# First loads from two queues, four square buffers and earlier splits in a one-core float32 encoder trunk

## The chip, the core and the metric

The kernel runs on one core of a Trainium2 chip. The time is the device time of one execution in microseconds (us). The profile is of one execution; its engines are PE (TensorE, the matrix engine), PEld (its weight loads), DVE (VectorE), ACT (ScalarE), POOL (GpSimd) and SP (SyncE, which here only issues transfers). A "q" behind an engine's name is its instruction queue, for instance SPq for the transfers that SP issues.

## What is computed

Two layers on 272 tokens (16 learned tokens ahead of 256) of width 1024, all in float32. Each layer is a half-step SwiGLU network, a mixer, and a second half-step SwiGLU network, each wrapped in two RMS norms. The mixer of the first layer is attention, that of the second a gated recurrence:

```python
for layer in range(2):
    g = norm_gains[layer]
    h = h + 0.5 * rms_norm(swiglu(rms_norm(h, g[0]), ffn_w_in[layer, 0], ffn_w_out[layer, 0]), g[1])
    hn = rms_norm(h, g[2])
    m = attention_mixer(hn, ...) if layer == 0 else recurrent_mixer(hn, ...)
    h = h + rms_norm(m, g[3])
    h = h + 0.5 * rms_norm(swiglu(rms_norm(h, g[4]), ffn_w_in[layer, 1], ffn_w_out[layer, 1]), g[5])
return h[:, 16:]
```

The recurrent mixer projects to a gate and to `xr`, runs a convolution of four taps over the tokens (`xc = conv_b + sum(xp[:, j:j + L] * conv_w[j])`), forms gates from `xc`, scans in both directions and projects back with `rec_w_out`.

## The kernel before

**Layout.** `h` lies transposed, 8 chunks of 128 features by 272 tokens. Each engine has its own program, written out by hand in the order in which it is to run, and semaphores join them; there is no scheduler. The program's blocks are `block.sync` (SP), `block.tensor` (PE), `block.scalar` (ACT), `block.vector` (DVE) and `block.gpsimd` (POOL).

**Products.** A float32 product is made of three matmuls (`product`, L508 to L510): weights and activations are each split in a rounded high part and a rest. ACT writes the high part of a weight unit (`high`, L1092, from `raw` to `wh`), DVE the rest (`low`, L1591, to `wl`), and then PE may use the unit. A unit is 1 MB (8 x 256 columns), there are four slots of `raw`, `wh` and `wl`, and SP loads a unit as soon as DVE has split what was in its slot. Activations are split in the same way: `xh` by ACT (`x_high`, L1098), `xl` by DVE (`low_x`, L1597).

**The start.** SP loads the tokens in six transfers, the left 512 columns ahead of the right 512 (`tokens(half)`, L432 to L434), and between and behind them the first weight unit in a quarter, a quarter and a half (L396), then unit after unit (L381). ACT's queue loads the learned tokens, the identity (`cst`) and the norm gains (L1528 to L1530). PE runs 13 products on zeros (L1059), transposes the tokens chunk by chunk (L1069; the gains, L1073, after the second chunk) into four banks, and then begins the first unit (`first_tiles`, L564 to L569, and the second unit at L547 to L550). ACT and DVE copy the transposed chunks to `h` (`take_h` L1537, `copy_h` L2154), split the unit in parts (`high_part` L1543, `low_part` L2150) and the activations.

**The end of a sub-layer.** The output projection ends in tiles of 128 features. For each, ACT squares it (`sqb`, two buffers) and scales it with the gain (`mg`), and DVE adds the squares up (`add_squares`, L1614, to `acc`). A square waits until the buffer is free, so for the addition two tiles back. The last square is not added by DVE: `mean_of_projection` (L970) multiplies `acc` and the last square with a matrix of 1/1024. ACT takes the root (`root_of_projection`, L1150), DVE adds the result to `h` (`residual`, L1641 to L1645). `mg_first` splits the first chunk of the scaled tile early (ACT L1108, DVE L1620), so that PE has work while the norm is finished (`first_chunk`, L527 to L531 for the second part of it). POOL multiplies `h` back by an older root in between (`restore`, L2205), and the root of the projection waits for that.

**Attention's output projection** (`projection(1, ...)`) has four units; DVE's turns are in `projection`: two additions, then a `low` of the next sub-layer's units. **The recurrent mixer** works through twelve units in the order of `REC_ORDER` ("x" and "e" are columns of `rec_w_in`, "g" gates); `conv` has 8 operations for a block of 256 features, two for each tap. **Its output projection** (`recurrent_out`) works in the order of `ROUT_PLAN`: tiles 0 to 5 by halves, then tiles 6 and 7, all in banks that ACT reads tile by tile; a tile from 4 on waits until ACT has emptied the tile that shared its bank.

Of the kernel before, what the change touches and what calls it, by code (L numbers as in the profile page):

```python
# [9 lines left out]
ALU = mybir.AluOpType  # L10
ACT = mybir.ActivationFunctionType
# [53 lines left out]
ROUT_SPLIT = 2  # L65
ROUT_PLAN = [(c, 0, 2) for c in range(KC)] + [(c, 2, 4) for c in range(KC)] + [(c, 4, 6) for c in range(6)] + [(c, 6, 8) for c in range(6)] + [(6, 4, 8), (7, 4, 8)]
# [88 lines left out]
def build(nc, x, meta, gains, ffn_in, ffn_out, w_qkv, q_gain, k_gain, w_o, rec_in, conv_w, conv_b,  # L155
          gate_w, gate_b, lam, rec_out, consts, out):
    ctx = ExitStack()
    with ctx:  # L158
# [108 lines left out]
        gates_used = sem("gates_used")  # L267
        xc_rounded, xc_split = sem("conv_rounded"), sem("conv_split")
# [3 lines left out]
        s_xin = [sem("left_tokens_landed"), sem("right_tokens_landed")]  # L272
# [87 lines left out]

        def conv_parts(n):

            v = split_a if n == 0 else split_b
            return v[:, 0], v[:, 1]
# [10 lines left out]
        def _(sp):  # L375
# [7 lines left out]
            def ffn(n):  # L383
# [45 lines left out]
            def tokens(half):  # L429

                cols = slice(D // 2 * half, D // 2 * half + D // 2)
                sp.dma_start(tok_in[META:TT, 0, cols], x[0:TT - META, cols]).then_inc(s_xin[half], 16)  # L432
                sp.dma_start(tok_in[0:TT, 1, cols], x[TT - META:2 * TT - META, cols]).then_inc(s_xin[half], 16)
                sp.dma_start(tok_in[0:L - 2 * TT, 2, cols], x[2 * TT - META:SEQ, cols]).then_inc(s_xin[half], 16)  # L434

# [10 lines left out]

            ffn(0)
# [55 lines left out]
        def _(pe):  # L503
# [582 lines left out]
        def _(act):  # L1086
# [320 lines left out]
            def recurrent():  # L1407
                def unit_high(what, freed, units):
                    high(U_REC + REC_ORDER.index(what), 0, KC, freed, units)

                def conv_high(n):
# [59 lines left out]
                unit_high("g1", (xr_done, 4), 1)  # L1471
# [794 lines left out]
```

## Time and profile before

| What | us |
|---|---|
| median of 3 runs | 1040.99 |
| lowest and highest | 1040.65, 1041.19 |
| the profiled execution | 1041.22 |
| its span from first to last instruction | 1039.3 |
| PE busy in the span | 1023.8 |
| DVE, ACT, POOL busy | 708.7, 562.5, 64.0 |

The profiled execution took 1.9 us more than its span, which lies before the first and behind the last instruction. Times in rows are counted from the start of the span. A row of the timeline is: start, length, engine, line, operation, tile written and tiles read, shape, count; in brackets the engine's idle time before it and what ended it. Consecutive instructions of one kind are merged to a row. A queued instruction's row can begin a little before its predecessor's ends, since engines are pipelined.

### The profile page before, as it was taken

How to read it: one execution, taken by the hardware profiler on the slowest of the kernel's cores; microseconds unless marked ns; L12 is line 12 of the kernel's file. 1: busy time of each engine (PE TensorE's matmuls, PEld its weight loads, DVE VectorE, ACT ScalarE, POOL GpSimd, SP SyncE). 2: the span in 40 equal slices, each digit the busy share in tenths (PEclk: the TensorE clock that was granted, in tenths of full speed). 3: DMA queues.
4: the chain of work that ended last, by engine and by line, in shares of the span. 5: the costliest groups of instructions: out<-in, count | busy, mean ns of one | idle time of the engine just before them, and what ended most of it. 6: DMA issues, size and time to landing. Idle time of an engine off the chain costs nothing. (4 is left out here: it accounts for less than half of the span.)

```text
span 1039.3 us, 20522 instructions
## 1 busy us (share of the span) xinstructions
PE 1023.8 (99%) x8308; PEld 999.9 (96%) x8308; DVE 708.7 (68%) x1040; ACT 562.5 (54%) x834; POOL 64.0 (6%) x62
## 2 busy tenths in 40 slices
PE   8999999999999999999999999999999999999997
PEld 8999999999889999999999999999999999999886
DVE  6766656488868866655478666654899987676652
ACT  6554454467875644445465444444679865544641
POOL 0000000008004000002100000030000030000000
PEclk9999999999999999999999999999999999999999
DMA  9754446635204355535655654367453736556531
GB/s 294 240 178 161 147 149 205 211 111 174 69 1 163 123 174 187 181 116 190 205 163 162 195 170 141 114 207 226 123 167 97 264 95 208 184 179 233 179 118 41
DMA packets 158175, 170.16 MB, mean 164 GB/s; under 512 B 3344, under 2 KB 150088, under 8 KB 158104
## 3 DMA queue, kind: packets, MB, share of 16 engines
q1 hardware_dynamic: 157720, 168.70, 50.1%
q8 instruction: 51, 0.84, 0.4%
q0 software_dynamic: 96, 0.28, 0.1%
q10 hardware_dynamic: 288, 0.18, 0.1%
q14 instruction: 20, 0.16, 0.1%
HBM read 167.82 MB, written 1.05 MB: 162 GB/s over the span
## 5 line engine op out<-in xcount | busy, mean ns | idle before, releaser
L1591 DVE TENSOR_TENSOR wl<-raw,wh 128x2048 fp32r<-128x2048 f32 (+3 forms) x166 | 346.6, 2108 | 141.5 <-ACT wh L1092 141.2
L508 PE MATMUL bank<-xh,wl 128*128 128x272 f32 (+1 forms) x1492 | 431.6, 289 | 0.2 <-DVE tmp L1707 0.2
L510 PE MATMUL bank<-xh,wh 128*128 128x272 f32 (+1 forms) x1492 | 428.5, 287 | 0.0
L509 PE MATMUL bank<-xl,wh 128*128 128x272 f32 (+1 forms) x1492 | 427.0, 286 | 0.0
L1092 ACT ACTIVATE wh<-raw 128x2048 fp32r<-128x2048 f32 (+2 forms) x165 | 284.2, 1746 | 104.5 <-PE bank L510 83.8
L508 PEld LDWEIGHTS bank<-xh,wl 128*128 128x128 f32 x1492 | 281.1, 188 | 2.1 <-issue 1.2
L510 PEld LDWEIGHTS bank<-xh,wh 128*128 128x128 f32 x1492 | 281.1, 188 | 0.0
L509 PEld LDWEIGHTS bank<-xl,wh 128*128 128x128 f32 x1492 | 281.0, 188 | 0.0
L509 PE MATMUL bank<-al,wh 128*128 128x272 f32 x528 | 152.2, 288 | 0.0
L508 PE MATMUL bank<-ah,wl 128*128 128x272 f32 x528 | 152.2, 288 | 0.0
L510 PE MATMUL bank<-ah,wh 128*128 128x272 f32 x528 | 151.4, 287 | 0.0
L1179 ACT ACTIVATE tmp<-tmp 128x272 f32<-128x272 f32 (+1 forms) x88 | 37.5, 428 | 207.6 <-DVE tmp L1706 207.4
L509 PEld LDWEIGHTS bank<-al,wh 128*128 128x128 f32 x528 | 99.3, 188 | 0.0
L510 PEld LDWEIGHTS bank<-ah,wh 128*128 128x128 f32 x528 | 99.2, 188 | 0.0
L508 PEld LDWEIGHTS bank<-ah,wl 128*128 128x128 f32 x528 | 99.2, 188 | 0.0
L1725 DVE TENSOR_TENSOR al<-tmp,ah 128x272 f32 (+3 forms) x88 | 38.2, 438 | 51.1 <-ACT ah L1184 50.5
L2205 POOL TENSOR_TENSOR h<-h,root 128x272 f32<-128x272 f32 (+1 forms) x32 | 39.4, 1267 | 538.5 <-DVE root L1630 409.6
L1706 DVE TENSOR_TENSOR tmp<-bank,r 128x272 f32<-128x272 f32 (+1 forms) x88 | 38.1, 433 | 46.1 <-PE bank L510 46.0
L1184 ACT ACTIVATE ah<-tmp 128x272 f32 (+3 forms) x88 | 37.4, 429 | 47.4 <-DVE tmp L1715 47.4
L1715 DVE TENSOR_TENSOR tmp<-tmp 128x272 f32<-128x272 f32 (+1 forms) x88 | 38.2, 438 | 13.6 <-ACT tmp L1179 10.1
L547 PE MATMUL bank<-xh,wl 128*128 128x272 f32 (+1 forms) x152 | 39.4, 287 | 0.2 <-DVE wl L2150 0.2
L548 PE MATMUL bank<-xh,wh 128*128 128x272 f32 (+1 forms) x152 | 39.3, 286 | 0.0
(246 smaller groups left out, 1191.2 us busy)
## 6 DMA issues: line engine op xcount, KB each, us to landing
raw<-in_ffn_w_in SPq DMA_DIRECT2D x87, 1024.0 KB, 5.8
raw<-in_ffn_w_out SPq DMA_DIRECT2D x24, 768.0 KB, 4.7
raw<-in_ffn_w_out SPq DMA_DIRECT2D x24, 640.0 KB, 3.9
raw<-in_ffn_w_out SPq DMA_DIRECT2D x10, 1024.0 KB, 5.0
raw<-in_rec_w_in SPq DMA_DIRECT2D x8, 1024.0 KB, 5.4
raw<-in_attn_w_qkv SPq DMA_DIRECT2D x6, 1024.0 KB, 5.0
raw<-in_attn_w_o SPq DMA_DIRECT2D x4, 1024.0 KB, 5.5
raw<-in_rec_gate_w SPq DMA_DIRECT2D x16, 256.0 KB, 3.7
```

What stands on the lines that cost most here:

```text
L508: pe.matmul(dst, b, mh, start=first, stop=False)
L509: pe.matmul(dst, a, ml, start=False, stop=False)
L510: return pe.matmul(dst, a, mh, start=False, stop=last)
L547: pe.matmul(dst, b, xh[:, k, t0:L], start=k == 0, stop=False)
L548: pe.matmul(dst, a, xh[:, k, t0:L], start=False, stop=False)
L1092: act.activation(wh[:, slot(u), 0:kn * 256], raw[:, slot(u), 0:kn * 256], ACT.Copy).then_inc(wh_ready, units)
L1179: act.activation(sl[:, b, t0:L], gp[:, b, t0:L], ACT.Silu).then_inc(silu_done, 1)
L1591: dve.tensor_tensor(wl[:, slot(u), 0:kn * 256], w, wh[:, slot(u), 0:kn * 256].bitcast(F32), ALU.subtract).then_inc(w_ready, units)
L1706: dve.tensor_tensor(gp[:, b, t0:L], bank[banks[0]][:, t0:L], r[:, t0:L], ALU.mult).then_inc(gate_scaled, 1)
L1715: dve.tensor_tensor(aa[:, b, t0:L], sl[:, b, t0:L], up[:, b, t0:L], ALU.mult).then_inc(a_full, 1)
L1725: dve.tensor_tensor(d, aa[:, b, t0:L], s, ALU.subtract).then_inc(a_ready, 1)
L2205: pool.tensor_tensor(h[:, c, t0:L], h[:, c, t0:L], root[:, t0:L], ALU.mult).then_inc(h_restored, 1)
```

## The change

**Start.** The tokens come in three transfers of whole rows ahead of all else on SP, under one semaphore. The first two quarters of the first unit move to ACT's queue, behind the identity and ahead of the gains. ACT and DVE split these quarters ahead of their copies of the transposed tokens (DVE's second quarter behind its third copy, and its fourth copy ahead of the first `low_x`).

**Attention's projection.** `mg_first` moves from the last turn to the second on ACT and DVE; DVE adds square 6 ahead of its last `low`.

**Convolution.** The first tap of the blocks 0 and 1 is made by ACT (`first_tap`), and DVE splits the gates' unit ahead of the other taps.

**Output projection of the recurrence.** Squares go through four buffers (two of `sqb`, two of `pad`), so that a square waits for the addition four tiles back; POOL begins its `restore` when the first output tile is done and not when the last product of scan and gate is.

```diff
+        def rout_square(m):
+
+            return (sqb[:, m % 2] if m % 4 > 1 else pad[:, m % 2, 0:L])[:, PROJ_T0[4]:L]
...
                 if n == 0:
-                    for k0, k1, done in ((0, 2, quarter_landed[0]), (2, 4, quarter_landed[1]), (4, 8, landed[0])):
-                        if k0 < 4:
-                            tokens(k0 // 2)
-                        sp.dma_start(raw[:, 0, 256 * k0:256 * k1].rearrange("p (k c) -> p k c", k=k1 - k0),
-                                     vin[:, k0:k1, 0:256]).then_inc(done, 16)
+                    sp.dma_start(raw[:, 0, 256 * 4:256 * 8].rearrange("p (k c) -> p k c", k=4), vin[:, 4:8, 0:256]).then_inc(landed[0], 16)
...
+            sp.dma_start(tok_in[META:TT, 0, :], x[0:TT - META, :]).then_inc(s_xin, 16)
+            sp.dma_start(tok_in[0:TT, 1, :], x[TT - META:2 * TT - META, :]).then_inc(s_xin, 16)
+            sp.dma_start(tok_in[0:L - 2 * TT, 2, :], x[2 * TT - META:SEQ, :]).then_inc(s_xin, 16)
             ffn(0)
...
                 if c == 0:
-                    pe.wait_ge(s_xin[0], 64)
-                if c == 4:
-                    pe.wait_ge(s_xin[1], 48)
+                    pe.wait_ge(s_xin, 64)
...
             def projection(pj, u0):
                 for g in range(4):
-                    if g == 3:
-                        mg_first(pj)
                     square_tile(pj, 2 * g, PROJ_BANKS[pj][g][0])
                     square_tile(pj, 2 * g + 1, PROJ_BANKS[pj][g][1])
+                    if g == 1:
+                        mg_first(pj)
...
+                def first_tap(n):
+
+                    act.wait_ge(xr_scaled, 2 * n + 2)
+                    for i in range(2):
+                        m = 2 * n + i
+                        act.activation(xc[:, n, i, :], pad[:, i, 0:L], ACT.Identity, scale=vec_b[:, V_CONVW + m:V_CONVW + m + 1],
+                                       bias=vec_b[:, V_CONVB + m:V_CONVB + m + 1]).then_inc(first_tapped, 1)
...
-                    act.wait_ge(acc_step, ACC * 4 + m + 1)
-                    act.activation(sqb[:, m % 2, t0:L], rout_dst(m), ACT.Square).then_inc(sq_ready, 1)
+                    act.wait_ge(acc_step, ACC * 4 + max(2, m - 1))
+                    act.activation(rout_square(m), rout_dst(m), ACT.Square).then_inc(sq_ready, 1)
...
             act.dma_start(cst[:, 0:C_ROT], consts[:, 0:C_ROT]).then_inc(s_in, 16)
+            first_in = ffn_in[0, 0].rearrange("(k p) c -> p k c", p=P)
+            for q in range(2):
+                act.dma_start(raw[:, 0, 512 * q:512 * q + 512].rearrange("p (k c) -> p k c", k=2),
+                              first_in[:, 2 * q:2 * q + 2, 0:256]).then_inc(quarter_landed[q], 16)
             act.dma_start(vrow[:, 0, :], gains.rearrange("l i (c p) -> (l i c) p", p=P)).then_inc(s_vin, 16)
...
             def projection(pj, u0):
-                for g in range(4):
-                    if g == 3:
-                        mg_first(pj)
+                for g in range(3):
                     add_squares(pj, 2 * g)
-                    if g < 3:
-                        add_squares(pj, 2 * g + 1)
+                    add_squares(pj, 2 * g + 1)
+                    if g < 2:
                         low(u0 + g + 4, 0)
                     if g == 0:
                         invert_root(pj)
+                    if g == 1:
+                        mg_first(pj)
+                add_squares(pj, 6)
+                low(u0 + 6, 0)
                 residual(pj)
...
                 if n == 4:
-                    pool.wait_ge(y_full, NB)
+                    pool.wait_ge(proj_done, 8 * n + 1)
```

PE's instructions keep their number and order. Three places show what moves elsewhere. The first is ACT at the start of the program: `quarter0` and `quarter1` are the first unit's quarters, `x_transposed` counts chunks that PE has transposed. Before, and then with the change:

```order
L1528 DMA tok_in<-in_meta_tokens 16x1024
L1529 DMA cst<-in_consts 128x131
L1530 DMA vrow<-in_norm_gains 96x128
L1162 ACT_TABLE_LOAD
L1162 ACTIVATE warm<-warm 1x1 [waits warm_set]
L1537 ACTIVATE h<-bank 128x272 [waits h_ready,x_transposed]
L1543 ACTIVATE wh<-raw 128x512 [waits first_unit_quarter0_landed]
L1098 ACTIVATE xh<-h,vec_a 128x272 [waits h_ready,vec_ready]
L1098 ACTIVATE xh<-h,vec_a 128x272 [waits h_ready] x2
L1543 ACTIVATE wh<-raw 128x512 [waits first_unit_quarter1_landed]
```

```order
L1534 DMA tok_in<-in_meta_tokens 16x1024
L1535 DMA cst<-in_consts 128x131
L1538 DMA raw<-in_ffn_w_in 128x2x256 x2
L1540 DMA vrow<-in_norm_gains 96x128
L1158 ACT_TABLE_LOAD
L1158 ACTIVATE warm<-warm 1x1 [waits warm_set]
L1553 ACTIVATE wh<-raw 128x512 [waits first_unit_quarter0_landed]
L1553 ACTIVATE wh<-raw 128x512 [waits first_unit_quarter1_landed]
L1547 ACTIVATE h<-bank 128x272 [waits h_ready,x_transposed]
L1094 ACTIVATE xh<-h,vec_a 128x272 [waits h_ready,vec_ready]
```

The gains are now the last of five transfers on ACT's queue, and ACT's first copy of `h`, on which PE's later transposes wait, stands behind both quarters.

The second is DVE in attention's output projection, from the additions 2 and 3 on (`acc`) to the first operation of the residual (`h<-h,root`). Before, and then with the change:

```order
L1614 TENSOR_TENSOR acc<-acc,sqb 128x272 [waits acc_step,sq_ready] x2
L1591 TENSOR_TENSOR wl<-raw,wh 128x2048 [waits wh_ready]
L1614 TENSOR_TENSOR acc<-acc,sqb 128x272 [waits acc_step,sq_ready] x2
L1591 TENSOR_TENSOR wl<-raw,wh 128x2048 [waits wh_ready]
L1620 SCALAR_TENSOR_TENSOR split_a<-mg,vec_a,split_a 128x272 [waits first_mg_rounded]
L1614 TENSOR_TENSOR acc<-acc,sqb 128x272 [waits acc_step,sq_ready]
L1641 TENSOR_TENSOR h<-h,root 128x272 [waits post_root,mg_ready,h_restored]
```

```order
L1624 TENSOR_TENSOR acc<-acc,sqb 128x272 [waits acc_step,sq_ready] x2
L1601 TENSOR_TENSOR wl<-raw,wh 128x2048 [waits wh_ready]
L1630 SCALAR_TENSOR_TENSOR split_a<-mg,vec_a,split_a 128x272 [waits first_mg_rounded]
L1624 TENSOR_TENSOR acc<-acc,sqb 128x272 [waits acc_step,sq_ready] x3
L1601 TENSOR_TENSOR wl<-raw,wh 128x2048 [waits wh_ready]
L1651 TENSOR_TENSOR h<-h,root 128x272 [waits post_root,mg_ready,h_restored]
```

The seventh addition is no longer behind the last `low` and the split, and that `low` now stands directly ahead of the residual.

The third is DVE in the recurrent mixer, block 0 (`pad` holds `xr`, `wl` is the unit "g0"). Before, and then with the change:

```order
L1972 TENSOR_TENSOR pad<-bank,r 128x272 [waits xr_done]
L1991 TENSOR_SCALAR xc<-pad,vec_b 128x272 [waits xr_scaled]
L1991 TENSOR_SCALAR xc<-pad,vec_b 128x272
L1995 SCALAR_TENSOR_TENSOR xc<-pad,vec_b,xc 128x272 [waits conv_step] x6
L1591 TENSOR_TENSOR wl<-raw,wh 128x2048 [waits wh_ready]
L2002 TENSOR_TENSOR split_a<-xc,split_a 128x544 [waits conv_rounded]
```

```order
L1984 TENSOR_TENSOR pad<-bank,r 128x272 [waits xr_done]
L1601 TENSOR_TENSOR wl<-raw,wh 128x2048 [waits wh_ready]
L2010 SCALAR_TENSOR_TENSOR xc<-pad,vec_b,xc 128x272 [waits first_tapped,xr_scaled]
L2010 SCALAR_TENSOR_TENSOR xc<-pad,vec_b,xc 128x272 [waits first_tapped]
L2010 SCALAR_TENSOR_TENSOR xc<-pad,vec_b,xc 128x272 [waits conv_step] x4
L2017 TENSOR_TENSOR split_a<-xc,split_a 128x544 [waits conv_rounded]
```

The `low` of the unit changes places with the taps, and the two operations of the first tap are gone from DVE.

## Rows read from the trace of the kernel before

**Rows 1.** The page, busy time of the engines in the span

```profile
PE 1023.8 (99%) x8308; PEld 999.9 (96%) x8308; DVE 708.7 (68%) x1040; ACT 562.5 (54%) x834; POOL 64.0 (6%) x62
```

**Rows 2.** PE's waits: whom for, total us, times, longest

```profile
PE bank L970 <- DVE acc L1614: 1.5, 2, 1.3
```

**Rows 3.** Stretches: length, busy time by engine, clock, DMA share, GB/s

```profile
3.00:6.00 3.00, 3.00 (x16) 3.00 (x15) 0.00 (x0) 0.64 (x2) 0.00 (x0) 1.00 1.06 240
6.00:9.00 3.00, 2.17 (x22) 1.99 (x20) 1.23 (x4) 1.05 (x3) 0.00 (x0) 1.00 1.07 232
9.00:12.00 3.00, 2.45 (x24) 2.45 (x25) 3.00 (x8) 2.92 (x7) 0.00 (x0) 1.00 1.10 344
...
10.74:23.64 12.90, 12.69 (x100) 12.26 (x99) 10.80 (x15) 12.16 (x22) 0.00 (x0) 1.00 1.09 348
23.64:264.00 240.36, 240.10 (x1948) 237.67 (x1946) 160.33 (x246) 126.87 (x187) 24.42 (x26) 1.00 0.55 177
```

**Rows 4.** The timeline of the start, all engines

```profile
1.84 5.29 PE L1059 MATMUL bank<-pad 128*128 128x128 f32 x26 [1.84 <-DVE pad L2145]
...
7.45 0.25 PE L1073 MATMUL bank<-cst,vrow 96*128 96x96 f32 x1
...
7.95 0.40 ACT L1537 ACTIVATE h<-bank 128x272 f32<-128x272 f32 x1 [4.29 <-PE bank L1069]
...
9.55 1.17 PE L1069 MATMUL bank<-cst,tok_in 96*128 96x96 f32 x12 [1.38 <-DMA tok_in<-in_x]
...
10.74 0.37 PE L564 MATMUL bank<-xh,wl 128*128 128x272 f32 x1
...
17.66 1.92 ACT L1092 ACTIVATE wh<-raw 128x2048 fp32r<-128x2048 f32 x1 [0.55 <-DMA raw<-in_ffn_w_in]
```

**Rows 5.** The timeline at the end of attention's output projection, by engine

```profile
323.73 2.78 DVE L1591 TENSOR_TENSOR wl<-raw,wh 128x2048 fp32r<-128x2048 f32 x1 [0.74 <-ACT wh L1092]
326.43 1.01 DVE L1620 SCALAR_TENSOR_TENSOR split_a<-mg,vec_a,split_a 128x272 fp32r<-128x272 f32 x1
327.36 0.99 DVE L1614 TENSOR_TENSOR acc<-acc,sqb 128x272 f32<-128x272 f32 x1
```

**Rows 6.** The same stretch, ACT, PE and POOL

```profile
327.17 0.40 ACT L1138 ACTIVATE sqb<-bank 128x272 f32<-128x272 f32 x1 [2.25 <-PE bank L510]
...
328.40 0.73 PE L970 MATMUL bank<-acc,cst 128*128 128x136 f32 x4 [1.27 <-DVE acc L1614]
...
317.19 10.86 POOL L2205 TENSOR_TENSOR h<-h,root 128x272 f32<-128x272 f32 x8 [55.42 <-DVE root L1630]
```

**Rows 7.** The timeline of the recurrent mixer around its first gates

```profile
762.14 0.78 DVE L1972 TENSOR_TENSOR pad<-bank,r 128x272 f32<-128x272 f32 x2
...
764.09 1.92 ACT L1092 ACTIVATE wh<-raw 128x2048 fp32r<-128x2048 f32 x1 [3.59 <-PE bank L510]
```

**Rows 8.** The timeline of the recurrence's output projection, by engine

```profile
831.10 0.38 ACT L1520 ACTIVATE sqb<-bank 128x256 f32<-128x256 f32 x1 [3.31 <-PE bank L970]
...
835.73 0.39 ACT L1520 ACTIVATE sqb<-bank 128x256 f32<-128x256 f32 x1 [2.70 <-DVE acc L1614]
...
841.99 0.38 ACT L1150 ACTIVATE root<-bank 128x256 f32<-128x256 f32 x1
...
828.88 5.02 DVE L1591 TENSOR_TENSOR wl<-raw,wh 128x2048 fp32r<-128x2048 f32 x2
...
834.69 5.81 DVE L1614 TENSOR_TENSOR acc<-acc,sqb 128x256 f32<-128x256 f32 x7
...
857.66 2.29 DVE L1591 TENSOR_TENSOR wl<-raw,wh 128x2048 fp32r<-128x2048 f32 x1
...
829.13 10.56 POOL L2205 TENSOR_TENSOR h<-h,root 128x256 f32<-128x256 f32 x8 [128.96 <-DVE tmp L2044]
```

**Rows 9.** PE in that stretch

```profile
836.53 3.84 PE L970 MATMUL bank<-tmp,rout_x 128*128 128x128 f32 x32 [1.00 <-ACT mg L1521]
840.56 0.71 PE L970 MATMUL bank<-acc,cst 128*128 128x128 f32 x4 [0.19 <-DVE acc L1614]
```

More of the change, by code:

```diff
@@ L65 @@
 ROUT_SPLIT = 2
+TAPPED = 2
 ROUT_PLAN = [(c, 0, 2) for c in range(KC)] + [(c, 2, 4) for c in range(KC)] + [(c, 4, 6) for c in range(6)] + [(c, 6, 8) for c in range(6)] + [(6, 4, 8), (7, 4, 8)]
@@ L267, in build @@
         gates_used = sem("gates_used")
+        first_tapped = sem("first_tapped")
         xc_rounded, xc_split = sem("conv_rounded"), sem("conv_split")
@@ L427, in last_out @@
                         sp.dma_start(dst, vout[:, 4 * j:4 * j + kn, 512 * half:512 * half + 512]).then_inc(landed[slot(u)], 16)
[L429 to L434, printed above, removed]
             def vectors():
@@ L1471, in recurrent @@
                 unit_high("g1", (xr_done, 4), 1)
+                first_tap(0)
                 unit_high("e0", (xr_done, 6), 1)
                 conv_high(0)
+                first_tap(1)
                 unit_high("e1", (xr_done, 8), 1)
@@ L1543, in high_part @@
                 act.activation(wh[:, slot(u), cols], raw[:, slot(u), cols], ACT.Copy).then_inc(done, 1)
+            high_part(0, 0, 2, (quarter_landed[0], 16), wh_half)
+            high_part(0, 2, 4, (quarter_landed[1], 16), wh_half)
             take_h(1)
-            high_part(0, 0, 2, (quarter_landed[0], 16), wh_half)
             act.wait_ge(vec_ready, 1)
@@ L1985, in conv @@
                     dve.wait_ge(xr_scaled, 2 * n + 2)
-                    for tap in range(CONVW):
+                    for tap in range(1 if n < TAPPED else 0, CONVW):
                         for i in range(2):
@@ L1993, in conv @@
                             else:
-                                dve.wait_ge(conv_step, 2 * (CONVW * n + tap) + i - 1)
+                                if tap == 1 and n < TAPPED:
+                                    dve.wait_ge(first_tapped, 2 * n + i + 1)
+                                else:
+                                    dve.wait_ge(conv_step, 2 * (CONVW * n + tap) + i - 1)
                                 dve.scalar_tensor_tensor(xc[:, n, i, :], pad[:, i, tap:tap + L], vec_b[:, v:v + 1], xc[:, n, i, :],
-                                                         ALU.mult, ALU.add).then_inc(conv_step, 1)
+                                                         ALU.mult, ALU.add).then_inc(conv_step, 2 if tap == 1 and n < TAPPED else 1)
                 def conv_low(n):
@@ L2061, in recurrent @@
                 x_scaled(0)
+                unit_low("g0", 1)
                 conv(0)
-                unit_low("g0", 1)
                 conv_low(0)
                 x_scaled(1)
+                unit_low("g1", 1)
                 conv(1)
-                unit_low("g1", 1)
                 conv_low(1)
@@ L2110, in recurrent_out @@
                 for m in range(7):
-                    add_squares(4, m)
+                    dve.wait_ge(sq_ready, 8 * 4 + m + 1)
+                    dve.wait_ge(acc_step, ACC * 4 + m + 2)
+                    dve.tensor_tensor(acc[:, PROJ_T0[4]:L], acc[:, PROJ_T0[4]:L], rout_square(m), ALU.add).then_inc(acc_step, 1)
                 residual(4)
@@ L2154, in copy_h @@
                 dve.tensor_copy(h[:, c, :], bank[4 + c % 4][:, 0:L]).then_inc(h_ready, 1)
+            low_part(0, 0, 2, (wh_half, 1), w_half)
             copy_h(0)
@@ L2161, in _ @@
             copy_h(3)
-            low_part(0, 0, 2, (wh_half, 1), w_half)
+            low_part(0, 2, 4, (wh_half, 2), w_half)
+            copy_h(4)
             dve.wait_ge(vec_ready, 1)
```

7 lines of the change are left out of this document (2 added, 5 removed).

## The prediction

> **What bounds the kernel now.** I read the page first, then who PE waits for, then a table of stretches, and only then the timelines of the few places where PE stands. PE is busy for 1023.8 of 1039.3 us, DVE for 708.7, ACT for 562.5 [rows 1]. A change that issues the same matmuls in the same order can therefore win nothing but PE's idle time, 15.5 us in all, and only the part of it that lies where the change acts. 1.84 of it lie ahead of the first warm-up product [rows 4], and more behind the last matmul; the change touches neither. Of what is left PE waits 1.5 us for `acc` in two waits [rows 2], 1.38 for the tokens [rows 4] and 1.0 for `mg` in the recurrence's output projection [rows 9]. So the gain has a ceiling of about 4 us plus what the start can be brought forward. A second view matters: the DMA engines are the bound of the first 18 us. They are busy throughout and move 232 to 240 GB/s while the tokens are among the traffic, 344 to 348 afterwards [rows 3]; at 17.66 ACT still waits for a weight unit [rows 4]. From 23.64 on they are busy half the time [rows 3], so nothing later hangs on them. PE itself has no slack at the start: it is busy 12.69 of 12.90 us from the first real matmul on [rows 3]. What its first matmul (10.74) is moved by, the end is moved by.
>
> About 0.2%, 2.1 us, is what a measurement of this kernel can tell from no change; the parts below are all smaller.
>
> **Attention's projection: 1.3 us won.** PE's products end about 327.1, and the mean over `acc` starts at 328.40 after 1.27 us idle [rows 6], since DVE first splits a unit (323.73 to 326.5), then `mg`'s first chunk (1.01 us) and then adds square 6 (0.99, to 328.35) [rows 5]. Square 6 is made by ACT long before, one tile (3.0 us) ahead of square 7 at 327.17, so at 324.5. With the change the order is split of `mg`, additions 4, 5, 6, then the unit. Additions here take 0.99 us beside POOL: from 321.1 on, when DVE is through with the unit before, 1.0 + 2 x 1.0 is 324.1, addition 6 waits for 324.5 and is done at 325.5. The mean over `acc` then starts with PE's last product, and the mean over square 7 (ready at 327.57) ends about 1.3 us earlier than before. What is late next: the unit is split from 325.5 to 328.3 (2.78) and stands directly ahead of the residual, which can start at about 328.7, when the root is there; POOL's restore ends at 317.19 + 10.86 = 328.05 [rows 6], and the new root wants to begin at about 328.3. Both are hidden by 0.2 to 0.4 us and no more. I take 1.3; bounds 0.9 (one of the covers is gone) and 1.4.
>
> **The convolution: nothing.** DVE is relieved of four operations, but PE does not wait there. Before, DVE has split `xc` and emptied the banks of the second x unit at 762.14 + 0.78 = 762.9, and PE finishes the unit ahead of the gates at about 764.05, which is what ACT's `high` waits for at 764.09 [rows 7]. 1.1 us of cover hides the whole part. The order of DVE is now unit, taps 1 to 3, then a wait for ACT's rounding of `xc`, which also stood ahead of the split before, so that the split comes within 0.1 us of where it was. ACT was idle for 3.59 us there, and its two taps fit in. If the cover were gone the price would be what the split is late by, at most the 2.28 us of a unit. Bounds: 0 and 0.3 lost.
>
> **The recurrence's output projection: 0.6 us won.** PE is idle for 1.0 us ahead of tile 6 (836.53), because it needs the third `mg`, which ACT makes behind the third square, and that waited 2.70 us for an addition [rows 8, 9]. With four buffers the third square is made at 833, and this stall goes. It does not all come back: `acc` is late next. DVE's chain is two units, the split of `mg` (0.9) and seven additions (5.81) [rows 8], it ends at 840.50, and it is the same work as before. What helps it is POOL. A restore's operations get in DVE's way: two units take 5.02 us beside it, where one takes 2.29 alone [rows 8]. POOL now starts at 831.1, with the first tile [rows 8], and the units cost about 0.5 us less. So `acc` is ready at 840.0 instead of 840.5, and the wait of the mean starts earlier and ends 0.5 earlier. The root (841.99) stood a little later still, because ACT split half a unit ahead of it; with the last product 1.1 us earlier that half is out of the way by 841.1. The root starts at about 841.4. POOL, started 2.0 us later, saves the 1.9 us that it stood behind the first unit and so ends at 840.2 instead of 839.7, in time for the root. I take 0.6; bounds 0 (POOL ends after the root wants to start: 831.1 + 10.56 = 841.7) and 1.2 (all of PE's idle).
>
> The Trainium skill, "SBUF — State Buffer", section "SBUF: two separate sides", says that DVE and GpSimd take their shared port pair as an exclusive lock for a whole instruction. The restore's time agrees: 10.56 us for eight operations beside DVE's units and additions [rows 8].
>
> **The start: 1.6 us lost.** The first tile needs the tokens (1.05 MB), the learned tokens, the identity and the gains (0.18) and the first unit's first half (0.52 MB), 1.75 MB. Before, its matmuls could start when the tokens and one quarter were in, 1.49 MB, and the right half of the tokens was in at 9.55, when PE's wait ended [rows 4]. While they waited, the left half had been transposed, the gains had been transposed at 7.45, and ACT's chain of copies and splits had begun at 7.95 [rows 4]. Now ACT copies nothing before both quarters are in, and the gains are behind them in the same queue, while SP's queue brings the tokens and then the unit's second half at the same time. 0.26 MB more at 0.24 MB per us [rows 3] is 1.1 us, so the last of these transfers is in at about 10.6 if the unit's second half takes no share, later if it does. I estimate that some of the slow rate goes, since weights and tokens are now mixed from the start, and put the quarters and gains at 10.1. Behind them come the gains' transposition, `vec_a`, the third and fourth copy (0.4 each), the last transpositions: the work from 7.45 to 9.2 and the last third of 9.55 to 10.74 in rows 4, about 2.2 us. The first real matmul is then at 12.3, 1.6 after 10.74. ACT's and DVE's chain is as late, so nothing behind it catches up.
>
> Bounds: if the tokens as whole rows moved at 0.345 MB per us from the start [rows 3], 1.75 MB would be in at 1.8 + 5.1, plus 0.8 to land, 7.7, and the first matmul at 9.9: 0.9 won. If the second half of the unit takes its full share (a further 0.52 MB at 0.345), the gains come 0.8 us later than I put them: 2.4 lost. I take 1.6, because the rate of rows 3 holds for the very traffic that is in question.
>
> The Trainium skill, "DMA: Bandwidth & Descriptors", section "Issuing engines are not separate DMA queues", speaks against this part: transfers that several engines issue run on the same 16 DMA engines, and a second issuer saves only issue time. By that rule two queues bring nothing sooner; by rows 3 the DMA engines are already full from 3 us on, so the trace agrees.
>
> **The sum.** -1.3 - 0.6 + 0 + 1.6 = -0.3 us against the profiled execution's 1041.22, which stands 0.2 above the median of 1040.99. Against the median: 1040.7.
>
> **The rivals.**
> - *The forecast, 0.57:* two stalls shortened, the start gives most of it back. 1040.7.
> - *Whole rows are what the start lacked, 0.23.* Six transfers of half rows become three of whole rows. If the halves are the cause of the slow 232 to 240 GB/s, the start wins 0.9 as worked out: -1.9 - 0.9 = -2.8, 1038.2. For it: the rate jumps to 344 when the tokens are through. Against: ACT's chain, which now starts with a wait for transfers that before stood behind other work.
> - *PE's clock falls in the longer pause, 0.12; this is the case that ends slower.* Before, the warm-up ends about 7.1, and PE's longest pause is 1.38 us [rows 4]; it ran at the full 2.4 GHz after it. Now PE has six transpositions between 7.1 and about 10.2 and otherwise waits for the gains. If that pause is long enough, the first unit runs at 1.2 GHz: in the warm-up a product of 128 columns took 5.29 / 26 = 0.20 us, at full clock one of 272 takes 240.36 / 1948 = 0.12 [rows 3, 4], so half of the time at the low clock is lost. With a low clock for as long as the warm-up, 4.5 us, that is 2.2 us: 1040.7 + 2.2 = 1042.9. It decides from the point where the pause is over 1.4 us by much.
> - *The covers are gone, 0.08.* POOL's restore (of 0.2 us of cover in one projection, a start 2 us later in the other) holds up both roots: -0.9 - 0 + 1.6 = +0.7, 1041.7.
>
> **How the numbers follow.** Faster than 1038.9 needs the second case or nearly: 0.22. Slower than 1043.1 needs the clock to fall with the start at its upper bound: 0.08. Within 0.2%: 0.70. The range takes in the second case's own value and the third's without the last tenth: 1038.2 to 1042.7.
>
> **What would show it.** Right: PE's mean over `acc` at the end of attention's projection follows the last product without a wait; tile 6 of the recurrence's projection starts without one, and 0.5 to 1 us of wait appears ahead of the mean over `acc`; the time from that projection's first tile to the root shrinks by 0.6; the gains' transposition comes after 9.5 and the first matmul of the unit after 11.5. Wrong: the first real matmul at or before 10.7; any wait of PE at the recurrent mixer's gates; a root that waits for POOL's `h`; a granted clock below 1 after the warm-up; a table load ahead of ACT's first tap.

## The result and the profile after

| What | before | with the change |
|---|---|---|
| median, us | 1041.18 | 1043.12 |
| lowest and highest | 1040.55, 1041.86 | 1042.32, 1043.95 |
| runs | 22 | 22 |
| span of the profiled execution | 1039.3 | 1040.6 |

The ratio is 1.0018, with a 95% interval of 1.0012 to 1.0024: the change costs 1.9 us. The forecast was 1040.7, and its range ended at 1042.7. The profiled execution of the changed kernel took 1042.40 and so is one of the shorter ones.

First, whom PE waits for with the change (engine, tile, line, releaser: total us, times, longest):

```profile
PE bank L1069 <- DMA vrow<-in_norm_gains: 2.2, 1, 2.2
PE bank L1057 <- DVE pad L2162: 1.8, 1, 1.8
PE bank L1065 <- DMA tok_in<-in_x: 1.5, 1, 1.5
...
PE bank L968 <- DVE acc L2128: 1.3, 1, 1.3
```

Of the two waits for `acc` in [rows 2] one is gone, that of attention's projection. A wait for the gains, 2.2 us, is new.

The timeline of the start with the change, PE and ACT:

```profile
1.84 4.74 PE L1057 MATMUL bank<-pad 128*128 128x128 f32 x26 [1.84 <-DVE pad L2162]
8.11 0.67 PE L1065 MATMUL bank<-cst,tok_in 96*128 96x96 f32 x6 [1.54 <-DMA tok_in<-in_x]
11.02 0.30 PE L1069 MATMUL bank<-cst,vrow 96*128 96x96 f32 x1 [2.24 <-DMA vrow<-in_norm_gains]
11.16 2.17 PE L1065 MATMUL bank<-cst,tok_in 96*128 96x96 f32 x18
...
13.49 0.57 PE L562 MATMUL bank<-xh,wl 128*128 128x272 f32 x1
...
8.90 0.63 ACT L1553 ACTIVATE wh<-raw 128x512 fp32r<-128x512 f32 x1 [4.14 <-DMA raw<-in_ffn_w_in]
10.51 0.63 ACT L1553 ACTIVATE wh<-raw 128x512 fp32r<-128x512 f32 x1 [0.98 <-DMA raw<-in_ffn_w_in]
11.05 0.38 ACT L1547 ACTIVATE h<-bank 128x272 f32<-128x272 f32 x1
```

Against [rows 4] the first real matmul stands at 13.49 and not at 10.74. The transpositions of two chunks lie between two pauses of 1.54 and 2.24 us. Stretches of the same time (length; busy time of PE, PEld, DVE, ACT, POOL; granted clock, DMA share, GB/s):

```profile
3.00:6.00 3.00, 3.00 (x20) 3.00 (x19) 0.00 (x0) 1.49 (x2) 0.00 (x0) 1.00 1.06 254
6.00:9.00 3.00, 1.24 (x12) 0.91 (x10) 0.00 (x0) 0.10 (x1) 0.00 (x0) 1.00 1.06 283
9.00:12.00 3.00, 0.98 (x12) 0.98 (x13) 1.63 (x4) 1.79 (x4) 0.00 (x0) 1.00 1.11 343
12.00:15.00 3.00, 3.00 (x18) 2.98 (x17) 3.00 (x9) 2.97 (x7) 0.00 (x0) 0.50 1.10 348
15.00:18.00 3.00, 3.00 (x24) 3.00 (x24) 2.94 (x6) 2.90 (x7) 0.00 (x0) 0.93 1.10 349
```

The DMA engines do move more than in [rows 3], 283 for 232 GB/s from 6 to 9 us, with whole rows of tokens beside quarters of the unit. But from 12 to 15 us the granted clock is 0.50, so PE runs at 1.2 GHz: it issues 18 matmuls in 3 us where it issues 24 or more at full clock. PE's matmuls are as many and in the same order in both kernels, so they can be compared one by one. The second product of the second unit comes 2.9 us later than before (20.59 for 17.70), and the difference stays there until attention's projection.

The end of attention's projection, DVE, then ACT and PE:

```profile
324.89 1.96 DVE L1624 TENSOR_TENSOR acc<-acc,sqb 128x272 f32<-128x272 f32 x2
327.48 1.03 DVE L1624 TENSOR_TENSOR acc<-acc,sqb 128x272 f32<-128x272 f32 x1 [0.64 <-ACT sqb L1134]
328.43 2.86 DVE L1601 TENSOR_TENSOR wl<-raw,wh 128x2048 fp32r<-128x2048 f32 x1
331.82 0.79 DVE L1651 TENSOR_TENSOR h<-h,root 128x272 f32<-128x272 f32 x2 [0.53 <-ACT root L1146]
...
331.29 0.40 ACT L1146 ACTIVATE root<-bank 128x272 f32<-128x272 f32 x1 [0.44 <-PE bank L968]
...
329.88 0.63 PE L968 MATMUL bank<-acc,cst 128*128 128x136 f32 x4
```

DVE waits for ACT's square and not the other way round. The mean (329.88) carries no wait, which in [rows 6] was 1.27 us. It comes 1.5 us later than before in a kernel that was 2.9 late, so 1.4 are won. The unit is split by 331.29, 0.53 ahead of the residual.

The recurrence's output projection, POOL, DVE, PE:

```profile
832.88 8.80 POOL L2222 TENSOR_TENSOR h<-h,root 128x256 f32<-128x256 f32 x8 [131.05 <-PE bank L968]
...
830.53 4.49 DVE L1601 TENSOR_TENSOR wl<-raw,wh 128x2048 fp32r<-128x2048 f32 x2
...
841.20 0.76 DVE L2128 TENSOR_TENSOR acc<-acc,sqb 128x256 f32<-128x256 f32 x1
...
842.02 0.71 PE L968 MATMUL bank<-acc,cst 128*128 128x128 f32 x4 [1.27 <-DVE acc L2128]
```

The wait ahead of tile 6 in [rows 9] is gone, and 1.27 us of wait stand ahead of the mean where there were 0.19. Both of DVE's units take 4.49 and not 5.02 us beside POOL [rows 8]. PE's part behind the root comes 1.2 us later than before, where it was about 1.65 late ahead of the projection: 0.4 won.

### The profile page after: what moved, and what is told of

It is laid out like the page before. It is cut to its first block and busy times, and to the rows that moved or that the text cites. A ratio compares the mean times of both kernels' runs of the same rounds, so it can differ in the third digit from the quotient of the medians.

```text
span 1040.6 us, 20522 instructions
## 1 busy us (share of the span) xinstructions
PE 1024.3 (98%) x8308; PEld 1000.9 (96%) x8308; DVE 707.6 (68%) x1036; ACT 564.5 (54%) x838; POOL 60.5 (6%) x62
## 5 line engine op out<-in xcount | busy, mean ns | idle before, releaser
L2222 POOL TENSOR_TENSOR h<-h,root 128x272 f32<-128x272 f32 (+1 forms) x32 | 35.8, 1155 | 541.2 <-DVE root L1640 410.1
```

## The experiments

Each is compared with the kernel before on the same chip; its median there is 1041.02 to 1041.10, and 1040.88 beside four of them (buffers alone, restore alone, whole rows, halves on two queues). "Offset" is by how much a matmul of PE starts later than the same one in the profiled execution before.

**The old start.** The changed kernel with the loads, waits and orders of the start of before.

```diff
+                    for k0, k1, done in ((0, 2, quarter_landed[0]), (2, 4, quarter_landed[1]), (4, 8, landed[0])):
+                        if k0 < 4:
+                            tokens(k0 // 2)
...
-            sp.dma_start(tok_in[META:TT, 0, :], x[0:TT - META, :]).then_inc(s_xin, 16)
```

> The changed kernel with the start of the kernel before. Theory A (the start alone loses, 2.9 us and more; attention's projection wins 1.3, the recurrence's output projection 0.4, the taps nothing): 1.7 us faster than the kernel before, ratio 0.9984, PE's first real matmul at 10.74 and the granted clock 0.999 in every execution. Theory B (a part behind the start costs something too, hidden in the one trace by the shift): within 0.5 us of the kernel before.

Measured: 1039.14 us (1038.99 to 1041.00, 11 runs), ratio 0.9985 (0.9976 to 0.9994). This version is faster than both kernels, by 1.9 and by 4.0 us. So the start alone turns a gain into a loss. Its longest pause of PE after the warm-up:

```profile
9.38 1.17 PE L1075 MATMUL bank<-cst,tok_in 96*128 96x96 f32 x12 [1.62 <-DMA tok_in<-in_x]
```

The granted clock was 1.00 behind it. The clock was not full in every execution, as Theory A had it: the one of 1041.00 us had a mean clock of 0.998.

**The new start alone**, in the kernel before:

```diff
+            for q in range(2):
+                act.dma_start(raw[:, 0, 512 * q:512 * q + 512].rearrange("p (k c) -> p k c", k=2),
+                              first_in[:, 2 * q:2 * q + 2, 0:256]).then_inc(quarter_landed[q], 16)
```

> The kernel before with the new start alone. Theory A: PE's first real matmul at 13.5, the second network's weight units from 26.5 on, and an end later by 2.9 us in executions with one stretch at the low clock (mean clock 0.998) and by 3.8 in those with two (0.996), median ratio 1.0032. Theory B: less than 2.5 us.

Measured: 1045.11 (1044.12 to 1045.63, 5 runs), ratio 1.0040 (1.0026 to 1.0053), 4.1 us lost. Its stretches:

```profile
9.00:12.00 3.00, 1.16 (x8) 1.16 (x9) 1.47 (x4) 1.37 (x4) 0.00 (x0) 0.77 1.10 340
12.00:15.00 3.00, 3.00 (x20) 3.00 (x19) 3.00 (x8) 2.72 (x6) 0.00 (x0) 0.50 1.11 350
15.00:18.00 3.00, 3.00 (x17) 3.00 (x17) 2.97 (x6) 2.90 (x8) 0.00 (x0) 0.60 1.10 348
```

Here the low clock lasts longer than in the profiled execution of the changed kernel (0.60 for 0.93 from 15 to 18 us). PE's offset grows from 3.4 us ahead of the first real matmul to 4.9 at 17.45 and settles at 4.1. This offset and the difference of the times are the same. Theory A had expected 2.9 or 3.8 us; the loss was larger than either.

**Attention's projection alone:**

```diff
-                    if g == 3:
-                        mg_first(pj)
...
+                    if g == 1:
+                        mg_first(pj)
```

> The kernel before with the new order of attention's projection alone. Theory A: 1.3 us faster (0.9988), no wait of PE ahead of the mean over acc. Rival (the stall returns as a wait for GpSimd's restore or for the last low): less than 0.5 us faster, and ACT's root or DVE's first operation of the residual shows the wait.

Measured: 1039.40 (1038.91 to 1040.17, 11 runs), ratio 0.9986 (0.9977 to 0.9995). The mean over `acc` now follows the last product without a wait:

```profile
326.90 0.62 PE L970 MATMUL bank<-acc,cst 128*128 128x136 f32 x4
```

The offset at this mean is -1.5 us, and -1.3 behind it. This part is the larger one of the change's gain.

**The taps alone**, with the gates' unit split ahead of them:

```diff
-                    for tap in range(CONVW):
+                    for tap in range(1 if n < TAPPED else 0, CONVW):
```

> The kernel before with the first taps on ACT and the gates' low ahead of the convolution, alone. Theory A: within 0.3 us of the kernel before, PE without a wait from 755 to 835. Rival (ACT's taps delay the rounding of xc or a gate's sigmoid): 0.5 us slower or more, with a wait of PE at the first gates.

Measured: 1041.12 (11 runs) for 1041.09 before, ratio 0.9999 (0.9990 to 1.0008). PE's offset does not move at the gates.

**The output projection of the recurrence**: both edits, then each of them.

```diff
-                    act.wait_ge(acc_step, ACC * 4 + m + 1)
-                    act.activation(sqb[:, m % 2, t0:L], rout_dst(m), ACT.Square).then_inc(sq_ready, 1)
+                    act.wait_ge(acc_step, ACC * 4 + max(2, m - 1))
+                    act.activation(rout_square(m), rout_dst(m), ACT.Square).then_inc(sq_ready, 1)
...
-                    pool.wait_ge(y_full, NB)
+                    pool.wait_ge(proj_done, 8 * n + 1)
```

> The kernel before with four square buffers and the later restore alone. Theory A: 0.4 us faster (0.9996): PE's 1.0 us ahead of tile 6 is gone and 1.3 us ahead of the mean over acc is new. Rival (the shift of the start made that stall, not DVE's chain): 1.0 us faster.

> The kernel before with only the four square buffers; POOL's restore starts where it did. The two parts together moved PE by -0.2 at the end of this projection, and the mean over acc then waited 1.27 us behind the last product. Theory F (the late restore is what frees DVE, the buffers only take the stall ahead of tile 6 away): tile 6 starts without a wait, the mean waits about 1.0 to 1.3 us, acc is ready at the same 840.5 as before, and the root moves by 0.1 or less; 1041.0. Theory G (the buffers do it all, since the additions start as early either way): the mean is as early as with both, PE -0.2 and 1040.7 to 1040.9.

> The kernel before with only POOL's restore started at the first output tile. Theory F: DVE's two units take 4.5 us and not 5.02, but the restore now lies beside the additions; the squares still go through two buffers, so tile 6 waits about 0.5 to 1.0 us as before and the mean follows with little wait; the root moves by -0.2 to 0. Theory G: nothing moves or the root comes later, 0 to +0.3. Both 1040.8 to 1041.3 in time; the place in the trace tells them apart.

Measured: both 1040.66 (ratio 0.9989 to 1.0007), buffers alone 1040.53 (0.9986 to 1.0005), restore alone 1040.65 (0.9989 to 1.0007). The times can't tell them apart, nor from the kernel before; the offsets, of one profiled execution each, can. Across the projection PE's offset falls by 0.4 with both, by 0.24 with the buffers, by 0.44 with the restore. DVE and PE with the buffers alone:

```profile
828.75 5.02 DVE L1595 TENSOR_TENSOR wl<-raw,wh 128x2048 fp32r<-128x2048 f32 x2
...
840.43 0.71 PE L974 MATMUL bank<-acc,cst 128*128 128x128 f32 x4 [1.45 <-DVE acc L2117]
```

And with the later restore alone:

```profile
828.83 4.49 DVE L1591 TENSOR_TENSOR wl<-raw,wh 128x2048 fp32r<-128x2048 f32 x2
...
834.11 6.14 DVE L1614 TENSOR_TENSOR acc<-acc,sqb 128x256 f32<-128x256 f32 x7
...
835.94 3.84 PE L970 MATMUL bank<-tmp,rout_x 128*128 128x128 f32 x32 [0.46 <-ACT mg L1521]
...
840.30 0.71 PE L970 MATMUL bank<-acc,cst 128*128 128x128 f32 x4 [0.52 <-DVE acc L1614]
```

Two things set the root. One is DVE's chain up to the last addition: the restore alone shortens the units by 0.53 and lengthens the additions by 0.33, so the mean starts 0.2 earlier; the buffers leave it where it was and only move PE's wait from tile 6 to the mean. The other is ACT, which before splits half a unit just ahead of the root: from the mean's start to the root's it is 1.43 us (840.56 to 841.99 [rows 8, 9]), and 1.20 with either edit. ACT with the buffers alone:

```profile
841.63 0.39 ACT L1154 ACTIVATE root<-bank 128x256 f32<-128x256 f32 x1 [0.92 <-PE bank L974]
```

So the buffers win the second part, the restore wins both, and together they win no more than the restore. Theory F had the owners right (with the buffers alone the mean is as late as before) and the sizes too small: it put at most 0.1 on the buffers and at most 0.2 on the restore.

**Gains ahead of the quarters**, and all else as changed:

```diff
+            act.dma_start(vrow[:, 0, :], gains.rearrange("l i (c p) -> (l i c) p", p=P)).then_inc(s_vin, 16)
             first_in = ffn_in[0, 0].rearrange("(k p) c -> p k c", p=P)
...
-            act.dma_start(vrow[:, 0, :], gains.rearrange("l i (c p) -> (l i c) p", p=P)).then_inc(s_vin, 16)
```

> The changed kernel with the gains moved ahead of the two quarters on ACT's queue. Theory C (what holds the start is that ACT copies nothing before both quarters are in; the gains' place matters little): PE's first real matmul at 13.2 instead of 13.5, the kernel 0.3 us faster than the changed one. Theory D (the gains' late landing at 10.98 holds the start): first matmul at or before 12.3, 1.2 us faster or more.

Measured: 1043.84 (1043.16 to 1044.81, 10 runs), ratio 1.0027 (1.0017 to 1.0036), no gain over the changed kernel, though both theories had it faster. PE:

```profile
11.83 0.46 PE L1065 MATMUL bank<-cst,tok_in 96*128 96x96 f32 x3 [2.87 <-DVE h L2171]
```

And the stretch from 12 to 15 us of the same kernel:

```profile
12.00:15.00 3.00, 2.68 (x17) 2.33 (x17) 2.43 (x6) 2.84 (x8) 0.00 (x0) 0.67 1.10 348
```

The gains are in at 7.8 us, but now PE waits 2.87 us for a bank: DVE's copy of `h` stands behind the split of the first quarter, which is in at 10.05. The wait has another name and is no shorter (2.24 us in the changed kernel).

**Gains first, and ACT and DVE in their order of before** (ACT's part of the edit; DVE's steps move back in the same way):

```diff
+            take_h(1)
             high_part(0, 0, 2, (quarter_landed[0], 16), wh_half)
-            high_part(0, 2, 4, (quarter_landed[1], 16), wh_half)
-            take_h(1)
...
+            high_part(0, 2, 4, (quarter_landed[1], 16), wh_half)
```

> As the one before, with ACT's and DVE's order of the first splits and copies as in the kernel before; the loads still come from two queues. Theory C: first real matmul at 11, a few tenths late against 10.74, and a wait at the second quarter; the granted clock stays at the full level; 2.3 us faster than the changed kernel in its better executions, about 1.3 faster than the kernel before. Theory E (two queues alone cost the start, whatever the order behind them): still over 1.5 us behind the old start, so slower than the kernel before.

Measured: 1041.10 (1040.61 to 1041.45, 11 runs), ratio 0.9999 (0.9990 to 1.0008). PE:

```profile
8.43 2.14 PE L1065 MATMUL bank<-cst,tok_in 96*128 96x96 f32 x18
...
11.45 0.39 PE L562 MATMUL bank<-xh,wl 128*128 128x272 f32 x1 [0.61 <-DVE wl L2167]
...
13.22 0.39 PE L562 MATMUL bank<-xh,wl 128*128 128x272 f32 x1 [0.51 <-DVE wl L2167]
```

And the stretch from 12 to 15 us of the same kernel:

```profile
12.00:15.00 3.00, 2.49 (x20) 2.27 (x19) 2.76 (x6) 2.97 (x7) 0.00 (x0) 1.00 1.10 348
```

From the tokens' landing on PE transposes without a pause and its clock stays at 1.00, but the quarters, in at 10.0 and 11.6, hold the unit up twice. The kernel is 2.7 us faster than with the new order and 2.0 slower than with the old start.

**Gains last, ACT and DVE in their order of before**, the fourth corner of the square:

```diff
+            take_h(1)
             high_part(0, 0, 2, (quarter_landed[0], 16), wh_half)
-            high_part(0, 2, 4, (quarter_landed[1], 16), wh_half)
-            take_h(1)
...
+            high_part(0, 2, 4, (quarter_landed[1], 16), wh_half)
```

> The changed kernel with ACT's and DVE's order of before at the start; the gains stay last on ACT's queue. With the gains first the new order gave 1043.84 and the old one 1041.10; the changed kernel (gains last, new order) 1043.12. If the order is what costs (theory O): the chunks that need no gain are copied while the gains are under way, PE's wait for the gains at 11.0 is still there, since their transposition stands behind the second chunk, but the chain behind is no longer than before: 1041.5 to 1042.3, with the clock as before or in one low stretch. If either of the two alone is enough (theory X): PE stands 1.5 + 2.2 us as in the changed kernel, the granted clock is 0.50 behind it in all runs, and the time is 1042.5 to 1043.5, the old order being worth less than 0.6 here.

Measured: 1043.49 (1042.49 to 1044.01, 11 runs), ratio 1.0021 (1.0012 to 1.0030). PE:

```profile
11.12 0.42 PE L1069 MATMUL bank<-cst,vrow 96*128 96x96 f32 x1 [2.26 <-DMA vrow<-in_norm_gains]
```

And the stretch from 12 to 15 us of the same kernel:

```profile
12.00:15.00 3.00, 3.00 (x19) 3.00 (x19) 2.89 (x7) 2.42 (x6) 0.00 (x0) 0.50 1.10 348
```

| | order of before | new order |
|---|---|---|
| gains first | 1041.10 | 1043.84 |
| gains last | 1043.49 | 1043.12 |

Theory X holds: either of the two is enough for a pause of over 2 us (2.24 to 2.87) and the low clock behind it, and the second costs nothing more. The pause ahead of it was 0.86 us in the fourth corner and not 1.5. To undo one alone does not help.

**More warm-up products**, the changed kernel with 30 instead of 13:

```diff
-WARM = 13
+WARM = 30
```

> The changed kernel with 30 warm-up products instead of 13, which end about 10.1, ahead of the gains. If the granted clock falls because PE rests from 6.6 to 11: no stretch at the low clock, the first unit's second half at the time that DVE's split allows (16.3 instead of 17.4), and 0.5 us faster than the changed kernel's better executions, 1.4 faster than the others, the two groups of times gone. If the clock falls for another cause: the same two groups as in the changed kernel.

Measured: 1041.72 (1041.59 to 1043.03, 11 runs), ratio 1.0007 (0.9998 to 1.0016). PE:

```profile
1.83 9.50 PE L1057 MATMUL bank<-pad 128*128 128x128 f32 x60 [1.83 <-DVE pad L2162]
11.16 0.64 PE L1065 MATMUL bank<-cst,tok_in 96*128 96x96 f32 x6
```

And the stretch from 12 to 15 us of the same kernel:

```profile
12.00:15.00 3.00, 2.98 (x28) 2.59 (x27) 2.64 (x8) 2.70 (x7) 0.00 (x0) 1.00 1.10 347
```

The products fill the pauses, the clock stays at 1.00, and 1.4 us come back though the gains still land at 10.7. In this profiled execution (1042.57) the warm-up ended later than the gains and so cost something itself. The two groups of times are gone but for two executions of eleven (1042.57 and 1043.03). So about 1.4 us of the loss is clock, and the rest, 2.6 against the old start, lateness.

**Whole rows or two queues.** First, all loads of the start on SP, tokens as whole rows, then quarter, quarter, half; then tokens in halves on SP and the quarters behind the gains on ACT. Both with the old order.

```diff
-                    sp.dma_start(raw[:, 0, 256 * 4:256 * 8].rearrange("p (k c) -> p k c", k=4), vin[:, 4:8, 0:256]).then_inc(landed[0], 16)
+                    for k0, k1, done in ((0, 2, quarter_landed[0]), (2, 4, quarter_landed[1]), (4, 8, landed[0])):
+                        sp.dma_start(raw[:, 0, 256 * k0:256 * k1].rearrange("p (k c) -> p k c", k=k1 - k0),
+                                     vin[:, k0:k1, 0:256]).then_inc(done, 16)
```

> The changed kernel with the order of ACT and DVE of before and all first loads on SP's queue: the tokens as three transfers of whole rows, then quarter, quarter, half. Against the kernel with the whole old start (1039.14) only the form and the order of the token transfers differ. With gains first, two queues and the old order of ACT and DVE it was 1041.10, 1.96 us more. Theory Q (the second queue costs it: the quarters share the DMA engines with tokens and gains and land late): tokens in at 7.2 to 7.8, quarters at 8.5 and 9.6, the first real matmul at 10.2 to 10.7, and 1038.6 to 1039.4. Theory R (whole rows cost it: no tile is transposed while the right half is under way, so ACT's and DVE's chain starts later): chain starts at 8.5 and not at 7.0, first real matmul at 11.2 or later and 1040.4 to 1041.2.

```diff
+                    tokens(0)
+                    tokens(1)
                     sp.dma_start(raw[:, 0, 256 * 4:256 * 8].rearrange("p (k c) -> p k c", k=4), vin[:, 4:8, 0:256]).then_inc(landed[0], 16)
```

> The changed kernel with the order of ACT and DVE of before and the tokens in halves on SP's queue, but the first two quarters on ACT's queue, behind the gains. Theory Q (the second queue costs it): the left half lands near 7, quarter 0 at 9 to 10, quarter 1 at 11 or later, PE waits for wl in the first unit, and 1040.4 to 1041.2. Theory R (whole rows cost it): 1039.0 to 1039.4, as with the old start.

Measured: whole rows on one queue 1040.00 (1039.86 to 1040.27, 11 runs), ratio 0.9992 (0.9983 to 1.0001); halves on two queues 1039.91 (1038.88 to 1041.08, 11 runs), ratio 0.9990 (0.9981 to 0.9999). PE with whole rows on one queue:

```profile
8.05 0.67 PE L1067 MATMUL bank<-cst,tok_in 96*128 96x96 f32 x6 [1.45 <-DMA tok_in<-in_x]
...
12.71 0.39 PE L564 MATMUL bank<-xh,wl 128*128 128x272 f32 x1 [0.51 <-DVE wl L2165]
```

PE with halves on two queues:

```profile
10.09 1.17 PE L1073 MATMUL bank<-cst,tok_in 96*128 96x96 f32 x12 [2.61 <-DMA tok_in<-in_x]
```

And the stretch from 12 to 15 us of the same kernel:

```profile
12.00:15.00 3.00, 3.00 (x15) 3.00 (x15) 2.85 (x6) 2.90 (x8) 0.00 (x0) 0.52 1.10 349
```

When the trace has each transfer landed (us, the profiled executions):

| | left, right tokens | gains | quarters | unit, second half |
|---|---|---|---|---|
| before | 6.2, 9.5 | 6.5 | 7.3, 10.1 | 11.6 |
| the change | 8.0 | 11.0 | 8.9, 10.5 | 11.1 |
| gains first, old order | 7.7 | 7.9 | 10.0, 11.6 | 10.4 |
| whole rows, one queue | 7.9 | 8.1 | 8.6, 9.4 | 10.9 |
| halves, two queues | 6.1, 10.1 | 6.3 | 8.2, 10.1 | 11.5 |

Neither theory is right alone: each costs 0.8 to 1.0 us against the old start (1039.14). With whole rows nothing waits for a transfer after 8.05; ACT's and DVE's chain starts 1.5 us later than with the old start, and PE leaves the start 1.0 later. With halves on two queues the right tokens come 0.7 us later, and the low clock is back in five of eleven executions (mean clock 0.997 or 0.998, 1040.6 to 1041.1; the other six 1038.9 to 1039.9). Whole rows on two queues, gains first, take 1.1 more than on one.

**Only what wins.** The earlier split of the projection and the later restore, in the kernel before:

```diff
+                    if g == 1:
+                        mg_first(pj)
...
-                    pool.wait_ge(y_full, NB)
+                    pool.wait_ge(proj_done, 8 * n + 1)
```

> The kernel before with only the earlier split of the projection and the later restore. If buffers and taps add nothing: PE is 1.3 earlier behind attention's projection and 0.45 more behind the recurrence's, together -1.8, 1039.1 to 1039.3, the same as with the old start and all else of the change (1039.14). If the buffers are worth what they gave alone (0.26 in the trace), 0.2 to 0.3 later than that, 1039.3 to 1039.5.

Measured: 1039.20 (1038.72 to 1039.89, 11 runs), ratio 0.9982 (0.9973 to 0.9991). It is as fast as the changed kernel with the old start, so buffers and taps add nothing. Attention's part alone (1039.40) already beats both kernels. The 0.2 us that the restore adds to it are within the intervals; the offset shows them as 0.44.

## Why the prediction was wrong

- **The start, put at 1.6 us lost with 2.4 as the bound, lost 3.8 to 4.0** (1043.12 against 1039.14 with the old start; 3.8 when each is set against the kernel before on its own chip). This is the step that failed, in three places: the landing, the work behind it, and the clock. The quarters and gains were put at 10.1 "if the unit's second half takes no share"; it took one. The gains landed at 10.98, behind the quarters in ACT's queue and beside what SP had issued. The work behind them took 2.5 us and not 2.2, with part of it at the low clock, and the first real matmul came at 13.49 and not 12.3. The Trainium skill, "DMA: Bandwidth & Descriptors", section "Queues, rings and completion order", says that each DMA engine round-robins between the queues it has work for, by packets. The landings agree: ACT's fifth transfer (the gains) is in at 10.98 and SP's fourth (half the unit) at 11.09, though ACT's five hold 0.7 MB and SP's four 1.6. In the profile's count of packets the two sets are nearly equal, 832 on ACT's queue and 823 on SP's. I had read only the total rate, which the change did raise, and not whose bytes come first. The upper bound was also reckoned wrong: 0.52 MB at 0.345 MB per us is 1.5 us and not 0.8, so by its own figures the bound was 3.1 us and would have held the 2.75 by which the first real matmul was late.
- **The clock's rival, given 0.12, came true, to all appearance in every execution.** All 22 runs have a mean clock of 0.996 to 0.998 (the kernel before, beside the experiments: 0.998 to 1.000, but for one execution of 113), and the runs fall in two groups, ten at 0.998 with 1042.3 to 1042.8 us and twelve at 0.996 or 0.997 with 1043.1 to 1044.0. It decided "over 1.4 us by much": the pauses were 1.54 and 2.24. I priced it at 2.2 and took it as independent of the start's lateness. It isn't: the later the gains, the longer the pause, so its chance belonged to the very term that I had placed nearest to its upper bound. The experiment with more warm-up products puts it at about 1.4 us. The rival's 2.2 came from 4.5 us at the low clock, which no row gives (the warm-up's row is 5.29 long); the profiled execution of the changed kernel had about 3.4. The rival's time, 1042.9, lies 0.2 from the measured one by luck: the clock cost less than it said and the lateness more, 2.4 to 2.6 for 1.6.
- **"Whole rows are what the start lacked", 0.23, fell.** The rate rose (283 for 232 GB/s), but even alone on one queue whole rows cost 0.9 us: the left half is no longer transposed meanwhile, and ACT's and DVE's chain starts 1.5 us later.
- **Attention's projection, 1.3 won, was right** in size (1.2 to 1.3 behind it in four traces) and in mechanism: 0.53 us lie between the unit's split and the residual, where about 0.4 was put. The other cover was larger than put. The restore took 9.04 us and not 10.86, and so ended 1.8 us earlier against PE's work.
- **The convolution, nothing, was right.**
- **The recurrence's projection, 0.6 won, was 0.4** with part of the mechanism as put: the stall ahead of tile 6 is gone, and `acc` is late next, with 1.27 us of wait where 0.5 to 1 was put. That POOL would be worth 0.5 to DVE's units was right (5.02 to 4.49); the additions beside it got 0.3 longer, which I hadn't counted. The runs also show that the buffers, on which I put the first half of the gain, add nothing to the restore. POOL was through at 841.68 and held up nothing (the root started at 843.21), so the last rival fell too. Its end had been put at 840.2; 839.7 + 2.0 - 1.9 is 839.8, and 841.68 less the 1.65 by which PE was late is 840.0.
- **The sum.** -1.3 - 0.4 + 0 + 3.8 to 4.0 is +2.1 to +2.3; measured +1.9, and the medians of the kernel before on the chips that the parts ran on lie up to 0.3 apart. With the start right the forecast would have been on the side of slower. The gain in the two projections (1.9 by the median) is real and is to be had without the start.

## What to carry to other kernels

When the transfer engines are full, ask not how fast all of it comes but which transfer the first dependent instruction needs and what is queued ahead of it, on its own queue and beside it; a small transfer that opens a chain goes first (worth 2.4 us here, once ACT and DVE stand in the old order). Behind an in-order engine, a wait for late data must not stand ahead of work whose data is there: here each of two such orders made a pause of over 2 us, and undoing one alone showed nothing. Where the change lengthens a pause of PE ahead of dense work, price the clock with it, in the same term.

## What was not expected of the hardware

- Pauses of 1.54 and 2.24 us with 0.67 us of transpositions between them were followed by a granted clock of 0.50 in the changed kernel; a single pause of 1.38 us (before) or 1.62 us (old start) wasn't, in the profiled executions. Of the kernel before, one of the 113 executions beside the experiments had a mean clock of 0.997 and took 1042.32. With the tokens in halves and the quarters on ACT's queue the profiled pause was 2.61 us, the granted clock behind it 0.52, and the mean clock was 0.997 or 0.998 in five executions of eleven.
- The time at the low clock differed between profiled executions. It was about 3.4 us in the changed kernel (0.50 and 0.93 in the stretches from 12 to 18 us, mean clock 0.998) and about 6.8 in the new start alone (0.77, 0.50 and 0.60 from 9 to 18 us, mean clock 0.996). The changed kernel's two groups of times, 0.9 us apart, have mean clocks like these, though only one execution of the faster group was profiled. What decides between them stays open.
- DVE's two units take 4.49 us beside a restore that starts 2 us later and 5.02 beside one that starts with them, and the restore itself 8.80 for 10.56. The seven additions take 0.33 more beside the later restore (6.14 for 5.81).
